# One matmul of 512 columns in place of two of 256 in four of seven Strassen steps: a decoder layer on Trainium2

## The chip, the cores and the metric

The kernel runs on one core of one Trainium2 chip. Its time is the device time of one execution in microseconds (us). Before the change three runs gave 1889.41, 1891.42 and 1900.57 us; the median is 1891.42 us. All data is float32, and the matmuls take their operands as `fp32r`, a form of float32 that TensorE reads directly. Every large product is made of three passes: each operand is split into a high part (rounded to `fp32r`) and a low part (what is left), and the product is high times high, plus high times low, plus low times high.

## The reference

One decoder layer over 512 tokens of width 2048: multi-head latent attention, a LayerNorm over the residual sum, then a dense MLP and another LayerNorm.

```python
h = layer_norm(ALPHA * h + mla_mixer(h, ...), ln_g[0, 0], ln_b[0, 0])
h = layer_norm(ALPHA * h + square(relu(h @ w1)) @ w2, ln_g[0, 1], ln_b[0, 1])
# h: 512 x 2048, w1: 2048 x 8192 (the up product), w2: 8192 x 2048 (the down product)
```

The change lies in the product of `h` with `w1`, called the up product here.

## The kernel before

The program runs in stages: the attention and its projections, the first LayerNorm (together the first third of the time), then the up product from about 592 us to 1237 us, then the down product and the second LayerNorm. There is no scheduler: the order of the work on each engine is the order in which the code writes it, and the engines meet through semaphores. TensorE (PE), VectorE (DVE) and ScalarE (ACT) each work through their own list and stop at the first wait that isn't met.

**The up product.** The 8192 columns of `w1` are taken in 32 pairs of 256 columns, that is two blocks of 128. The first two pairs are plain products. The other 30 (`UP_PAIRS - PLAIN`) use the Strassen-Winograd scheme: seven block products, steps 0 to 6, where a plain 2 x 2 block product needs eight. In one step a left operand (a block of `h`, or a sum of blocks, 1024 deep and 256 tokens wide, in SBUF as a high part `up_hi` and a low part `up_lo`) meets a weight block of 1024 x 128 (high part in `w_hi`, low part in `w_lo`, four slots each). The 1024 deep sum is eight chunks of 128 (`HK`), with three matmuls of 256 columns to a chunk (`product`, lines 1580, 1584 and 1585), so a step is 24 matmuls. The weights are the stationary operand, the tokens the moving one. The results of steps 0, 2, 4 and 6 add up in the one PSUM bank `i % 2`, step 1 goes to bank 2, steps 3 and 5 to bank 3.

**Around it, once per pair.**
- SyncE loads the four weight blocks b11, b12, b21, b22 (`up_loads`). DVE makes four sums of them (`up_t1` to `up_t4`, lines 1201 to 1219).
- ACT rounds each step's weights to `w_hi` (`up_weights`, line 701), and DVE subtracts to get `w_lo` (`up_rest`, line 1184). PE starts a step when its `w_lo` is there.
- ACT copies three partial results from PSUM into `kept` (`keep_product`, line 724): bank `i % 2` after step 0 and after step 2, and bank 3 after step 3. PE waits for them before step 2, step 4 and step 5, since those steps write over what is copied.
- DVE adds the final sums into `hidden` (`c_block`, line 1227, three times). The fourth block, c21, is what stands in bank `i % 2` after step 6: ACT applies the Relu as it reads it (`c21`, line 729).
- ACT applies Relu to the other three blocks (line 734, 768 columns) and squares all four (line 740, 1024 columns). DVE then makes the four sums and differences that the down product needs (`hidden_sums`, lines 1232 to 1237). ACT rounds seven blocks to `h_hi` (`hidden_hi`, line 747, 1792 columns) and stores it, DVE makes `h_lo` (`hidden_lo`, line 1244), and ACT issues its store. This work on pair i - 1 is done while PE is in pair i.

The functions that the change touches follow; `(i, n)` is the pair and the number of the part.

Of the kernel before, what the change touches and what calls it, by code (L numbers as in the profile page):

```python
# [4 lines left out]
P = 128  # L5
# [44 lines left out]
STEPS = 7  # L50
# [52 lines left out]
def mla_mlp_program(nc, xT, x, w, w_up, w_down, const, gain, ln, out):  # L103
# [3 lines left out]
    with ExitStack() as ctx:  # L107
# [69 lines left out]
        up_act = [None] * STEPS  # L177
        for step, left in enumerate(STEP_OF):
            up_act[left] = tuple(sb(f"up_{part}{left}", [P, HK, HT], f32r, at=base + (UP_ACT_AT[step] + 8 * i) * KB)
                                 for i, part in enumerate(("hi", "lo")))  # L180
# [11 lines left out]
        kept = sb("kept", [P, 3, HT], at=base + 144 * KB)  # L192
# [63 lines left out]
        p_kept, c21_made, c_made = sem("p_kept"), sem("c21_made"), sem("c_made")  # L256
        h_relu, h_made, h_sums = sem("h_relu"), sem("h_made"), sem("h_sums")
# [243 lines left out]
        def _(act):  # L501
# [219 lines left out]
            def keep_product(i, n, of, after):  # L721

                act.wait_ge(up_unit, up_steps(i, after - 1))
                act.activation(kept[:, n, :], of[:, 0:HT], ACT.Copy).then_inc(p_kept, 1)

            def c21(i):

                act.wait_ge(up_unit, up_steps(i, STEPS - 1))
                act.activation(hidden[:, 0, :], bank[:, i % 2, 0:HT], ACT.Relu).then_inc(c21_made, 1)

            def relu_hidden(i):

                act.wait_ge(c_made, 3 * (i - PLAIN) + 3)
                act.activation(hidden[:, 1:4, :], hidden[:, 1:4, :], ACT.Relu).then_inc(h_relu, 1)

            def square_hidden(i):

                act.wait_ge(h_relu, i - PLAIN + 1)
                act.wait_ge(c21_made, i - PLAIN + 1)
# [24 lines left out]
            def up_pair(i):  # L764

                relu_hidden(i - 1)
                c21(i - 1)
                square_hidden(i - 1)
                act.wait_ge(up_t_made, 4 * (i - PLAIN) + 3)
                up_weights(i, 2, b11[i % 2])  # L770
                act.wait_ge(up_t_made, 4 * (i - PLAIN) + 2)
                up_weights(i, 3, b12)
                keep_product(i, 0, bank[:, i % 2, :], 1)
# [7 lines left out]
                keep_product(i, 1, bank[:, i % 2, :], 3)  # L781
                act.wait_ge(up_t_made, 4 * (i - PLAIN) + 4)
                up_weights(i, 6, b21[i % 2])
                keep_product(i, 2, bank[:, 3, :], 4)
# [10 lines left out]
            def plain_pairs():  # L795
# [27 lines left out]
                keep_product(PLAIN, 0, bank[:, 0, :], 1)  # L823
# [6 lines left out]
                keep_product(PLAIN, 1, bank[:, 0, :], 3)  # L830
# [5 lines left out]
                keep_product(PLAIN, 2, bank[:, 3, :], 4)  # L836
# [73 lines left out]
            for n in range(4):  # L910
                down_weights(0, n)
            relu_hidden(last)
            c21(last)
# [306 lines left out]

# [863 lines left out]
```

## Time and profile before

| | before |
|---|---|
| median of three runs | 1891.42 us |
| profiled execution, its own time | 1892.82 us |
| span of the profile | 1890.7 us |
| PE busy | 1837.9 us (97%), 11120 matmuls |
| DVE busy | 1366.3 us (72%) |
| ACT busy | 889.1 us (47%) |
| mean granted TensorE clock | 0.991 |

The span goes from the first to the last instruction of the profiled execution. PE is busy when any matmul is between its start and its modelled end; matmuls are pipelined, so neighbours overlap, and what a matmul takes of PE's time is the distance from its start to the next one's start, not its duration. The same holds for DVE and ACT to a lesser degree: the next instruction starts a little before the last one's recorded end. The clock column PEclk gives the granted clock as a share of 2.4 GHz.

### The profile page before, as it was taken

What the parts mean: (1) busy time and instruction counts of PE and PEld (TensorE: products, weight loads), DVE (VectorE), ACT (ScalarE), POOL (GpSimd) and SP (SyncE); (2) the same over time, 40 slices, a digit from 0 to 9 for tenths busy, and PEclk for the clock granted to TensorE, in tenths of its full rate; (3) what the DMA queues carried; (4) which work ended last, traced back from release to release, by engine and by line L of the source; (5) the groups of instructions that cost most, each with busy time, mean ns of one, the idle gap of its engine ahead of it and who ended that gap; (6) DMA issues with size and microseconds to landing.
All of it is one profiled execution on the core that took longest, in us unless ns stands there. A gap on an engine that the chain in (4) does not pass through costs nothing.

```text
span 1890.7 us, 28438 instructions
## 1 busy us (share of the span) xinstructions
PE 1837.9 (97%) x11120; PEld 1647.0 (87%) x11120; DVE 1366.3 (72%) x1680; ACT 889.1 (47%) x1136; POOL 282.9 (15%) x118
## 2 busy tenths in 40 slices
PE   8999999999999999999999999989999999999994
PEld 6889898988888999999999999977887888788883
DVE  3054545521128888888888888878999999999997
ACT  5255655532217656656656556533433334333434
POOL 5342232324431000000000000000111122100003
PEclk9999999999999999999999999999999999999998
DMA  6222111133234564564564554686465564654812
GB/s 225 79 80 77 56 67 55 67 138 107 100 139 147 172 223 172 195 221 167 200 216 167 206 210 167 221 317 265 174 236 202 196 254 179 234 221 170 319 67 89
DMA packets 112719, 321.30 MB, mean 170 GB/s; under 512 B 7184, under 2 KB 64656, under 8 KB 95760
## 3 DMA queue, kind: packets, MB, share of 16 engines
q1 hardware_dynamic: 53280, 256.92, 36.2%
q10 hardware_dynamic: 59376, 63.59, 10.1%
q8 instruction: 32, 0.52, 0.1%
q14 instruction: 31, 0.25, 0.0%
HBM read 253.38 MB, written 67.11 MB: 170 GB/s over the span
## 4 chain that ended last, share of the span: by engine, by line
PE 86%; DVE 7%; issue 3%; DMA 1%; ACT 1%; POOL 1%; SPq 0%; POOLq 0%; ACTq 0%; DVEq 0%
PE bank L1580 28%; PE bank L1584 28%; PE bank L1585 28%; DVE w_lo L1312 2%; DMA d_b<-down_weights 1%; DVE acc L1372 1%; PE bank L1726 1%; DVE d_b L1347 1%; POOL w_lo L453 0%; DVE acc L1382 0%; PE bank L1612 0%; POOL acc L497 0%; ACT acc L935 0%; PE bank L1821 0%; PE bank L1718 0%
## 5 line engine op out<-in xcount | busy, mean ns | idle before, releaser
L1580 PE MATMUL bank<-up_hi,w_hi 128*128 128x256 f32 x1808 | 512.6, 284 | 3.2 <-DVE w_lo L1190 2.8
L1584 PE MATMUL bank<-up_lo,w_hi 128*128 128x256 f32 x1808 | 512.3, 283 | 0.0
L1585 PE MATMUL bank<-up_hi,w_lo 128*128 128x256 f32 x1808 | 512.3, 283 | 0.0
L1580 PE MATMUL bank<-w_hi,down_act 128*128 128x512 f32 x896 | 352.0, 393 | 13.6 <-DVE w_lo L1312 5.9
L904 ACT ACTIVATE w_hi<-d_b 128x1024 fp32r<-128x1024 f32 x192 | 201.5, 1060 | 321.8 <-PE bank L1585 251.9
L1580 PEld LDWEIGHTS bank<-up_hi,w_hi 128*128 128x128 f32 x1808 | 347.6, 192 | 3.9 <-DVE w_lo L1190 3.3
L1584 PE MATMUL bank<-w_lo,down_act 128*128 128x512 f32 x896 | 350.0, 391 | 0.0
L1585 PE MATMUL bank<-w_hi,down_act 128*128 128x512 f32 x896 | 349.9, 390 | 0.0
L1585 PEld LDWEIGHTS bank<-up_hi,w_lo 128*128 128x128 f32 x1808 | 347.8, 192 | 0.0
L1584 PEld LDWEIGHTS bank<-up_lo,w_hi 128*128 128x128 f32 x1808 | 347.8, 192 | 0.0
L1312 DVE TENSOR_TENSOR w_lo<-d_b,w_hi 128x1024 fp32r<-128x1024 f32 x190 | 251.7, 1359 | 24.1 <-ACT w_hi L904 24.1
L701 ACT ACTIVATE w_hi<-up_b 128x1024 fp32r<-128x1024 f32 x180 | 187.0, 1054 | 159.4 <-PE bank L1585 131.7
L453 POOL TENSOR_TENSOR w_lo<-raw,w_hi 128x1024 fp32r<-128x1024 f32 x82 | 198.0, 2417 | 355.5 <-ACT w_hi L510 355.3
L1580 PEld LDWEIGHTS bank<-w_hi,down_act 128*128 128x128 f32 x896 | 169.0, 189 | 56.8 <-issue 14.5
L1184 DVE TENSOR_TENSOR w_lo<-up_b,w_hi 128x1024 fp32r<-128x1024 f32 x180 | 216.9, 1218 | 1.4 <-ACT w_hi L701 1.4
L1585 PEld LDWEIGHTS bank<-w_hi,down_act 128*128 128x128 f32 x896 | 168.9, 189 | 35.4
L1584 PEld LDWEIGHTS bank<-w_lo,down_act 128*128 128x128 f32 x896 | 168.9, 189 | 34.2
L478 POOL TENSOR_TENSOR residual<-residual,ln_rows 128x1024 f32<-128x1024 f32 x8 | 36.2, 4525 | 1002.4 <-DMA residual<-rows_kept 1002.4
L510 ACT ACTIVATE w_hi<-raw 128x1024 fp32r<-128x1024 f32 x82 | 86.7, 1058 | 148.2 <-PE bank L1580 115.6
L1372 DVE TENSOR_TENSOR acc<-acc,bank 128x512 f32<-128x512 f32 x202 | 130.0, 679 | 12.4 <-PE bank L1585 12.1
L1138 DVE SCALAR_TENSOR_TENSOR rows<-rows,bank 128x512 f32<-128x512 f32 x16 | 11.0, 686 | 136.5 <-PE bank L1585 136.5
L1580 PE MATMUL bank<-w_hi,act_hi 128*128 128x512 f32 x256 | 99.9, 390 | 0.0
(168 smaller groups left out, 2782.0 us busy)
## 6 DMA issues: line engine op xcount, KB each, us to landing
up_b<-up_weights SPq DMA_DIRECT2D x128, 512.0 KB, 4.8
d_b<-down_weights SPq DMA_DIRECT2D x64, 1024.0 KB, 5.3
down_act<-acts_kept SPq DMA_DIRECT2D x56, 1024.0 KB, 5.0
raw<-weights SPq DMA_DIRECT2D x82, 512.0 KB, 3.2
acts_kept<-h_hi ACTq DMA_DIRECT2D x32, 896.0 KB, 5.8
acts_kept<-h_lo ACTq DMA_DIRECT2D x32, 896.0 KB, 6.6
x_raw<-x_t SPq DMA_DIRECT2D x8, 512.0 KB, 7.7
rows<-x_rows ACTq DMA_DIRECT2D x4, 1024.0 KB, 7.9
```

Of the source, the lines that this page charges most:

```text
L453: pool.tensor_tensor(w_lo[:, s, :], raw[:, s % RAWS, :], w_hi[:, s, :].bitcast(f32), ALU.subtract)\
L478: pool.tensor_tensor(part, part, ln_rows[:, 0, cols], ALU.mult).then_inc(residual_gained, 1)
L510: act.activation(w_hi[:, s, :], raw[:, s % RAWS, :], ACT.Copy).then_inc(w_hi_made, 1)
L701: act.activation(w_hi[:, UP_SLOT[u], :], source[:, :], ACT.Copy).then_inc(up_hi, 1)
L904: act.activation(w_hi[:, DOWN_SLOT[n], :], source[:, ab, :], ACT.Copy).then_inc(down_hi, 1)
L1184: dve.tensor_tensor(w_lo[:, s, :], source[:, :], w_hi[:, s, :].bitcast(f32), ALU.subtract).then_inc(up_lo, 1)
L1312: dve.tensor_tensor(w_lo[:, DOWN_SLOT[n], :], source[:, ab, :], w_hi[:, DOWN_SLOT[n], :].bitcast(f32), ALU.subtract).then_inc(made, 1)
L1347: dve.tensor_tensor(d_b11[:, ab, :], d_t3[:, ab, :], d_b11[:, ab, :], ALU.add).then_inc(down_t_made, 1)
L1372: dve.tensor_tensor(part, part, of, ALU.add).then_inc(evicted, 1)
L1580: first_pass = pe.matmul(out_, a_hi, b_hi, start=start, stop=False, skip_group_check=more)
L1584: pe.matmul(out_, a_hi, b_lo, start=False, stop=False, skip_group_check=more)
L1585: return pe.matmul(out_, a_lo, b_hi, start=False, stop=stop, skip_group_check=more)
```

## The change

In steps 0, 2, 4 and 6 the high weights now pass once over both parts of the left operand. The two parts already lie one after the other in SBUF, so a tensor `up_both` names them as one, and a single matmul of 512 columns writes high times high into the lower half of the PSUM bank and high times low into the upper half. The low weights then pass over the high part alone, into the lower half, as before. A chunk of such a step is so two matmuls (512 and 256 columns) instead of three of 256. Steps 1, 3 and 5 stay as they were.

The two halves of bank `i % 2` have to be added. ACT now copies the upper half to `kept` after steps 0, 2 and 6 (`keep_half`, in place of the two copies of the whole result and of the Relu of c21), and DVE adds the lower half to it: `keep_halves(i, 0)` after step 0, `keep_halves(i, 1)` after step 2, `c21` after step 6. In `c_block(i, 1)` after step 4 DVE first adds the upper half to the kept product of step 3 and then the lower half. PE waits for `keep_halves` where it waited for the copy. The Relu on ACT takes all four blocks.

```diff
-            def keep_product(i, n, of, after):
-                act.wait_ge(up_unit, up_steps(i, after - 1))
-                act.activation(kept[:, n, :], of[:, 0:HT], ACT.Copy).then_inc(p_kept, 1)
-
-            def c21(i):
-                act.wait_ge(up_unit, up_steps(i, STEPS - 1))
-                act.activation(hidden[:, 0, :], bank[:, i % 2, 0:HT], ACT.Relu).then_inc(c21_made, 1)
+            def keep_p5(i):
+                act.wait_ge(up_unit, up_steps(i, 3))
+                act.activation(kept[:, 2, :], bank[:, 3, 0:HT], ACT.Copy).then_inc(p_kept, 1)
+
+            def keep_half(i, n):
+                act.wait_ge(up_unit, up_steps(i, (0, 2, 6)[n]))
+                act.activation(kept[:, (0, 1, 3)[n], :], bank[:, i % 2, HT:2 * HT], ACT.Copy).then_inc(half_kept, 1)
             def relu_hidden(i):
                 act.wait_ge(c_made, 3 * (i - PLAIN) + 3)
-                act.activation(hidden[:, 1:4, :], hidden[:, 1:4, :], ACT.Relu).then_inc(h_relu, 1)
+                act.wait_ge(c21_made, i - PLAIN + 1)
+                act.activation(hidden[:, 0:4, :], hidden[:, 0:4, :], ACT.Relu).then_inc(h_relu, 1)
...
             def up_pair(i):
-                relu_hidden(i - 1)
-                c21(i - 1)
-                square_hidden(i - 1)
+                keep_half(i - 1, 2)
                 act.wait_ge(up_t_made, 4 * (i - PLAIN) + 3)
                 up_weights(i, 2, b11[i % 2])
+                relu_hidden(i - 1)
+                square_hidden(i - 1)
+                keep_half(i, 0)
                 act.wait_ge(up_t_made, 4 * (i - PLAIN) + 2)
                 up_weights(i, 3, b12)
-                keep_product(i, 0, bank[:, i % 2, :], 1)
                 hidden_hi(i - 1)
...
+            keep_half(last, 2)
             relu_hidden(last)
-            c21(last)
             square_hidden(last)
...
+            def keep_halves(i, n):
+                dve.wait_ge(half_kept, 3 * (i - PLAIN) + n + 1)
+                dve.tensor_tensor(kept[:, n, :], kept[:, n, :], bank[:, i % 2, 0:HT], ALU.add).then_inc(halves_kept, 1)
             def c_block(i, n):
                 dve.wait_ge(up_unit, up_steps(i, after - 1))
-                dve.wait_ge(p_kept, 3 * (i - PLAIN) + keeps)
+                if n == 1:
+                    dve.wait_ge(p_kept, i - PLAIN + 1)
+                    dve.tensor_tensor(kept[:, 2, :], bank[:, of, HT:2 * HT], kept[:, 2, :], ALU.add).then_inc(c22_half, 1)
+                    dve.wait_ge(c22_half, i - PLAIN + 1)
+                else:
+                    dve.wait_ge(halves_kept, 2 * (i - PLAIN) + keeps)
                 dve.tensor_tensor(hidden[:, at, :], bank[:, of, 0:HT], kept[:, keep, :], ALU.add).then_inc(c_made, 1)
+            def c21(i):
+                dve.wait_ge(half_kept, 3 * (i - PLAIN) + 3)
+                dve.tensor_tensor(hidden[:, 0, :], kept[:, 3, :], bank[:, i % 2, 0:HT], ALU.add).then_inc(c21_made, 1)
...
             for i in range(PLAIN, UP_PAIRS):
                 ahead = i < UP_PAIRS - 1
                 if i > PLAIN:
+                    up_rest(i, 2)
+                    keep_halves(i, 0)
                     hidden_sums(i - 1)
-                    up_rest(i, 2)
                     up_rest(i, 3)
                     hidden_lo(i - 1)
                     up_rest(i, 4)
...
                 c_block(i, 0)
                 if i > PLAIN:
                     up_t4(i)
+                    keep_halves(i, 1)
                     up_rest(i, 5)
...
                     c_block(i, 2)
                     up_t2(i + 1)
+                    c21(i)
                     up_rest(i + 1, 1)
                 else:
                     c_block(i, 2)
+                    c21(i)
                     down_rest(0, 0)
                     down_t3(0)
...
             def up_products(u, parity, ready=None):
+                    if u in (1, 3, 5):
+                        last = product(bank[:, b, 0:HT], w_hi[:, s, cols], w_lo[:, s, cols], a_hi[:, k, :], a_lo[:, k, :],
+                                       u in (1, 3) and k == 0, k == HK - 1, more)
+                    else:
+                        pe.matmul(bank[:, b, :], w_hi[:, s, cols], up_both[STEP_OF[u]][:, :, k, :],
+                                  start=u == 0 and k == 0, stop=k == HK - 1, skip_group_check=True)
+                        last = pe.matmul(bank[:, b, 0:HT], w_lo[:, s, cols], a_hi[:, k, :], start=False, stop=k == HK - 1,
+                                         skip_group_check=True)
                 last.then_inc(up_unit, 1)
...
-                pe.wait_ge(p_kept, 3 * (i - PLAIN) + 1)
+                pe.wait_ge(halves_kept, 2 * (i - PLAIN) + 1)
                 up_products(2, parity, (up_act_lo, 6) if first else None)
...
-                pe.wait_ge(p_kept, 3 * (i - PLAIN) + 2)
+                pe.wait_ge(halves_kept, 2 * (i - PLAIN) + 2)
                 up_products(4, parity, (up_act_lo, 12) if first else None)
```

The order on ACT from the end of one pair into the next. Before, the Relu and the Square of the finished pair come first, and the first copy to `kept` stands after both weights:

```order
L734 ACTIVATE hidden<-hidden 128x768
L729 ACTIVATE hidden<-bank 128x256
L740 ACTIVATE hidden<-hidden 128x1024
L701 ACTIVATE w_hi<-up_b_0_101 128x1024
L701 ACTIVATE w_hi<-up_b_98 128x1024
L724 ACTIVATE kept<-bank 128x256
L747 ACTIVATE h_hi<-hidden 128x1792
```

And in the change:

```order
L731 ACTIVATE kept<-bank 128x256
L702 ACTIVATE w_hi<-up_b_0_94 128x1024
L737 ACTIVATE hidden<-hidden 128x1024
L742 ACTIVATE hidden<-hidden 128x1024
L731 ACTIVATE kept<-bank 128x256
L702 ACTIVATE w_hi<-up_b_91 128x1024
L749 ACTIVATE h_hi<-hidden 128x1792
```

The rounding of step 2's weights moved ahead of the Relu and the Square, and the copy after step 0 ahead of step 3's weights.

The order on DVE over the same place, up to the sum `up_t4` (line 1219) and what follows it. Before:

```order
L1232 TENSOR_TENSOR hidden<-hidden 128x256
L1233 TENSOR_TENSOR hidden<-hidden 128x256
L1235 TENSOR_TENSOR hidden<-hidden 128x256
L1237 TENSOR_TENSOR hidden<-hidden 128x256
L1184 TENSOR_TENSOR w_lo<-up_b_1_104,w_hi 128x1024
L1184 TENSOR_TENSOR w_lo<-up_b_98,w_hi 128x1024
L1244 TENSOR_TENSOR h_lo<-hidden,h_hi 128x1792
L1184 TENSOR_TENSOR w_lo<-up_t_99,w_hi 128x1024
L1227 TENSOR_TENSOR hidden<-bank,kept 128x256
L1219 TENSOR_TENSOR up_b_1_105<-up_b_1_105,up_b_1_104 128x1024
L1184 TENSOR_TENSOR w_lo<-up_b_1_103,w_hi 128x1024
```

In the change line 1227 is `keep_halves`, lines 1236 and 1240 are `c_block`, and line 1221 is `up_t4`; step 2's `w_lo` stands just ahead of the first row:

```order
L1227 TENSOR_TENSOR kept<-kept,bank 128x256
L1250 TENSOR_TENSOR hidden<-hidden 128x256
L1251 TENSOR_TENSOR hidden<-hidden 128x256
L1253 TENSOR_TENSOR hidden<-hidden 128x256
L1255 TENSOR_TENSOR hidden<-hidden 128x256
L1186 TENSOR_TENSOR w_lo<-up_b_91,w_hi 128x1024
L1262 TENSOR_TENSOR h_lo<-hidden,h_hi 128x1792
L1186 TENSOR_TENSOR w_lo<-up_t_92,w_hi 128x1024
L1240 TENSOR_TENSOR hidden<-bank,kept 128x256
L1221 TENSOR_TENSOR up_b_0_95<-up_b_0_95,up_b_0_94 128x1024
L1227 TENSOR_TENSOR kept<-kept,bank 128x256
L1186 TENSOR_TENSOR w_lo<-up_b_1_96,w_hi 128x1024
```

The two `keep_halves` are new. The second one, for which PE waits before step 4, stands behind the whole row of work on the pair before, behind step 4's `w_lo` and behind `up_t4`.

The order on DVE where the up product ends, in the change (line 1330 is the down product's `down_rest`, line 1343 its `down_t3`):

```order
L1236 TENSOR_TENSOR kept<-bank,kept 128x256
L1240 TENSOR_TENSOR hidden<-bank,kept 128x256 x2
L1245 TENSOR_TENSOR hidden<-kept,bank 128x256
L1330 TENSOR_TENSOR w_lo<-d_b_114,w_hi 128x1024 x2
L1343 TENSOR_TENSOR d_t_117<-d_b_0_115,d_b_113 128x1024 x2
```

The new c21 (line 1245) stands ahead of the down product's first low weights; before, these followed the last `c_block` directly.

## Rows read from the trace of the kernel before

**Rows 1.** The page's first part: busy us, share of the span and instructions.

```profile
PE 1837.9 (97%) x11120; PEld 1647.0 (87%) x11120; DVE 1366.3 (72%) x1680; ACT 889.1 (47%) x1136; POOL 282.9 (15%) x118
```

**Rows 2.** Windows, up product: us; busy PE, PEld, DVE, ACT, POOL; clock; DMA share; GB/s.

```profile
700.00:1200.00 500.00, 500.00 (x4169) 500.00 (x4168) 424.45 (x473) 294.06 (x348) 0.00 (x0) 1.00 0.56 196
```

**Rows 3.** Timeline of PE: 256 columns 24 matmuls apart; 512 columns 9 apart.

```profile
start us, us, engine line op out<-in xcount [idle before <-releaser]
1014.92 0.28 PE L1580 MATMUL bank<-up_hi,w_hi 128*128 128x256 f32 x1
...
1017.80 0.28 PE L1580 MATMUL bank<-up_hi,w_hi 128*128 128x256 f32 x1
...
449.87 0.39 PE L1585 MATMUL bank<-w_hi,act_lo 128*128 128x512 f32 x1
...
451.91 0.39 PE L1585 MATMUL bank<-w_hi,act_lo 128*128 128x512 f32 x1
```

**Rows 4.** Timeline of ACT from the end of one pair into the next.

```profile
1015.12 0.38 ACT L729 ACTIVATE hidden<-bank 128x256 f32<-128x256 f32 x1 [1.03 <-PE bank L1585]
1015.60 1.06 ACT L740 ACTIVATE hidden<-hidden 128x1024 f32<-128x1024 f32 x1
1016.57 1.99 ACT L701 ACTIVATE w_hi<-up_b 128x1024 fp32r<-128x1024 f32 x2
1018.46 0.36 ACT L724 ACTIVATE kept<-bank 128x256 f32<-128x256 f32 x1
1018.72 1.69 ACT L747 ACTIVATE h_hi<-hidden 128x1792 fp32r<-128x1792 f32 x1
```

**Rows 5.** Timeline of DVE over the same stretch.

```profile
1016.69 0.43 DVE L1232 TENSOR_TENSOR hidden<-hidden 128x256 f32<-128x256 f32 x1 [1.75 <-ACT hidden L740]
...
1017.82 0.42 DVE L1237 TENSOR_TENSOR hidden<-hidden 128x256 f32<-128x256 f32 x1
1018.16 2.35 DVE L1184 TENSOR_TENSOR w_lo<-up_b,w_hi 128x1024 fp32r<-128x1024 f32 x2
1020.44 2.02 DVE L1244 TENSOR_TENSOR h_lo<-hidden,h_hi 128x1792 fp32r<-128x1792 f32 x1
1022.39 1.22 DVE L1184 TENSOR_TENSOR w_lo<-up_t,w_hi 128x1024 fp32r<-128x1024 f32 x1
1023.52 0.41 DVE L1227 TENSOR_TENSOR hidden<-bank,kept 128x256 f32<-128x256 f32 x1
1023.86 1.21 DVE L1219 TENSOR_TENSOR up_b<-up_b,up_b 128x1024 f32<-128x1024 f32 x1
```

**Rows 6.** Timeline where PE waits for a `w_lo` and starts again.

```profile
586.30 2.36 DVE L1190 TENSOR_TENSOR w_lo<-up_b,w_hi 128x1024 fp32r<-128x1024 f32 x2 [3.94 <-ACT w_hi L693]
...
587.58 0.19 PEld L1580 LDWEIGHTS bank<-up_hi,w_hi 128*128 128x128 f32 x1 [2.89 <-DVE w_lo L1190]
587.59 0.39 PE L1580 MATMUL bank<-up_hi,w_hi 128*128 128x256 f32 x1 [2.65 <-DVE w_lo L1190]
...
587.81 0.28 PE L1584 MATMUL bank<-up_lo,w_hi 128*128 128x256 f32 x1
```

**Rows 7.** The page's DMA issues: count, KB each, us to landing.

```profile
up_b<-up_weights SPq DMA_DIRECT2D x128, 512.0 KB, 4.8
```

**Rows 8.** Timeline of ACT and DVE where the down product begins.

```profile
1236.94 2.01 ACT L904 ACTIVATE w_hi<-d_b 128x1024 fp32r<-128x1024 f32 x2 [1.81 <-PE bank L1585]
...
1234.35 2.35 DVE L1312 TENSOR_TENSOR w_lo<-d_b,w_hi 128x1024 fp32r<-128x1024 f32 x2
1239.64 1.23 DVE L1325 TENSOR_TENSOR d_t<-d_b,d_b 128x1024 f32<-128x1024 f32 x1 [2.95 <-DMA d_b<-down_weights]
```

**Rows 9.** Windows behind the wait of Rows 6, and around one of 1.63 us.

```profile
588.00:592.00 4.00, 4.00 (x24) 4.00 (x24) 3.65 (x7) 3.04 (x5) 0.00 (x0) 0.60 0.91 290
...
1283.00:1287.00 4.00, 2.37 (x11) 1.72 (x10) 4.00 (x6) 2.00 (x2) 0.00 (x0) 1.00 0.57 240
```

**Rows 10.** Timeline of PE: that wait of 1.63 us.

```profile
1284.94 0.50 PE L1580 MATMUL bank<-w_hi,down_act 128*128 128x512 f32 x1 [1.63 <-DVE w_lo L1312]
```

More of the change, by code:

```diff
@@ L174, in mla_mlp_program @@
         rows = sb("rows", [P, TT, D], at=base + 80 * KB)
-        up_act = [None] * STEPS
+        up_act, up_both = [None] * STEPS, [None] * STEPS
         for step, left in enumerate(STEP_OF):
-            up_act[left] = tuple(sb(f"up_{part}{left}", [P, HK, HT], f32r, at=base + (UP_ACT_AT[step] + 8 * i) * KB)
-                                 for i, part in enumerate(("hi", "lo")))
+            up_both[left] = sb(f"up_act{left}", [P, 2, HK, HT], f32r, at=base + UP_ACT_AT[step] * KB)
+            up_act[left] = up_both[left][:, 0], up_both[left][:, 1]
         a21 = up_act[S3]
@@ L780, in up_pair @@
                 store_hidden(i - 1, 1)
-                keep_product(i, 1, bank[:, i % 2, :], 3)
+                keep_half(i, 1)
                 act.wait_ge(up_t_made, 4 * (i - PLAIN) + 4)
                 up_weights(i, 6, b21[i % 2])
-                keep_product(i, 2, bank[:, 3, :], 4)
+                keep_p5(i)
                 if i < UP_PAIRS - 1:
@@ L822, in plain_pairs @@
                 up_weights(PLAIN, 3, b12)
[L823 removed]
+                keep_half(PLAIN, 0)
                 hidden_hi(0)
@@ L829, in plain_pairs @@
                 store_hidden(0, 1)
-                keep_product(PLAIN, 1, bank[:, 0, :], 3)
+                keep_half(PLAIN, 1)
                 plain_square(1)
@@ L1504, in _ @@
             up_rest(PLAIN, 3)
+            keep_halves(PLAIN, 0)
             hidden_lo(0)
@@ L1508, in _ @@
             up_rest(PLAIN, 5)
+            keep_halves(PLAIN, 1)
             hidden_sums(1)
@@ L1846, in up_products @@
                 a_hi, a_lo = up_act[STEP_OF[u]]
-                dst = bank[:, (parity, 2, parity, 3, parity, 3, parity)[u], 0:HT]
+                b = (parity, 2, parity, 3, parity, 3, parity)[u]
+                more = u in (2, 4, 5, 6)
                 for k in range(HK):
@@ L1851, in up_products @@
                     cols = slice(P * k, P * k + P)
-                    last = product(dst, w_hi[:, s, cols], w_lo[:, s, cols], a_hi[:, k, :], a_lo[:, k, :],
-                                   u in (0, 1, 3) and k == 0, k == HK - 1, u in (2, 4, 5, 6))
+                    if u in (1, 3, 5):
[6 more added lines that the diff above has]
+                                         skip_group_check=True)
                 last.then_inc(up_unit, 1)
```

10 lines of the change are left out of this document (5 added, 5 removed).

## The prediction, made before the changed kernel was run

> **What bounds the kernel now.** I read the page's busy shares first: PE is busy for 97% of the span, DVE for 72%, ACT for 47% [rows 1]. An average over stages decides nothing, so the windows of the up product came next. In the 500 us from 700 to 1200 PE has no gap at all, at full clock, while DVE works 85% of the time and ACT 59% [rows 2]. There only the distance between two matmuls counts, and the timeline of PE gives it. Matmuls of 256 columns: 24 of them start in 2.88 us, 0.120 us each, and that is one step. Matmuls of 512 columns: 9 in 2.04 us, 0.227 us each [rows 3]. One pair is seven steps, 7 x 2.88 = 20.16 us. Last I laid the timelines of ACT and DVE beside it, since the change puts DVE between PE and PE [rows 4, 5]. DVE is idle for 1.75 us before `hidden_sums`, as it waits for the Square; then it has unbroken work up to `up_t4`. The slack there is large: step 4's `w_lo` is done at 1022.39 + 1.22 = 1023.61, and step 4 begins on PE at 1014.92 + 4 x 2.88 = 1026.44. PE waits for nobody because each thing it needs comes more than a microsecond early. So the question is whether this stays true.
>
> **PE's own work.** A merged pair of matmuls costs 0.227 in place of 0.240 us. The price is from contiguous moving operands; in the change the 512 columns are two runs of 256. That form is not in the trace. Its lower bound is 0.227 us; the upper bound is that nothing is gained, 0.240 us. I take 0.227, since it is the row of the same column count. A changed step has eight chunks of 0.227 + 0.120 us: 2.77 us, 0.11 us less than 2.88. Four such steps make 0.44 us a pair, 13.2 us in 30 pairs. That is all the change can give: 0.7% of the time.
>
> The Trainium skill ("TensorE: Matmul & The Clock Gate", Back-to-back issue gap) gives a warm matmul N / 2.4 ns plus a fixed 2.5 ns, so a merge would save only 2.5 ns: 30 x 32 x 2.5 ns = 2.4 us in all, an estimate from that page. The trace does not agree, as 256 columns take 120 ns where the rule gives 109; by the rule the changed step would be 2.86 us and my sum below 1929 us.
>
> **DVE's and ACT's work.** DVE gets four more additions of 256 columns in a pair: two `keep_halves`, a second one in `c_block(i, 1)`, and c21, which was ACT's. Each holds DVE for 0.34 us (1023.52 to 1023.86, [rows 5]), 1.4 us together with 0.1 us for the addition that waits for the one ahead. DVE's busy 0.85 x 20.16 = 17.1 us becomes 18.6, and PE's pair would be 19.72. So DVE is not full. ACT trades a Relu and three copies for four copies and gets a wider Relu: nearly nothing, hidden by its 40% of idle time. By busy time alone the change would win.
>
> **The new chain.** PE may start step 4 only when `keep_halves(i, 1)` is done, and that stands on DVE behind everything that belongs to the pair before, as the order of DVE in the change shows. I walk it with starts from [rows 4, 5]. Time 0 is 1015.12, when a pair's step 6 has released ACT; PE's next pair starts at -0.20 (1014.92).
> - ACT: copy of the half at 0.00. The next instruction follows a copy after 0.26 (1018.46 to 1018.72): step 2's `w_hi` at 0.26. Two `w_hi` are 0.945 apart: Relu at 1.21. It is now 1024 columns wide, which I price as the Square, 1.06 us: end 2.27. The Square waits for it, 0.10 after its end (1015.50 to 1015.60): 2.37. What follows the Square comes 0.97 later: the copy after step 0 at 3.34, end 3.72. Step 0 ended at 2.77, so PE isn't what it waits for.
> - DVE: meanwhile c21 at 0.41, step 1's `w_lo` at 0.75 (done 1.97, wanted at 2.57), step 2's `w_lo` at 1.88. Then it waits for that copy: `keep_halves(i, 0)` at 3.75, and `hidden_sums` at 4.09. Before, they began at 1.57: 2.5 us later, of which 1.1 is a `w_lo` that moved ahead. The four take 1.55 to the end of the last (1016.69 to 1018.24): 5.64.
> - ACT: `h_hi` at 5.67, 1.69 long, end 7.36. Before, it began at 3.60. DVE did two `w_lo` while it ran; now one is left to do (5.56 to 6.69), and DVE stands still until 7.39.
> - DVE: `h_lo` at 7.39; 1.95 later (1020.44 to 1022.39) step 4's `w_lo` at 9.34; 1.13 later `c_block(i, 0)` at 10.47; 0.34 later `up_t4` at 10.81; 1.13 later `keep_halves(i, 1)` at 11.94. With the 0.42 us of such an addition it ends at 12.36.
> - PE: the only start after a wait in this stage shows the weight load 0.06 after the `w_lo` (first of two, 586.30 + 1.22 = 587.52, to 587.58), the matmul 0.01 later, and the second matmul 0.22 behind it in place of 0.12 [rows 6]. Step 4 starts at 12.43 and loses 0.10.
>
> Without the wait it would start at -0.20 + 2.77 + 2.88 + 2.77 + 2.88 = 11.10. **PE stands 12.43 + 0.10 - 11.10 = 1.43 us in each pair**, 0.44 is saved, and the net is +0.99 us. It does not work itself off: every link from 0.00 on hangs on the end of step 6, so the next pair starts the same walk. Steps 4 to 6 take 8.42 us and DVE catches up: after `keep_halves` come three long instructions, step 6's `w_lo` being done at 15.76, wanted at 18.2.
>
> Other waits stay hidden. Step 2 wants `keep_halves(i, 0)` at 5.45, it ends at 4.17. Step 4's own `w_lo` ends at 10.56. Step 3's `w_lo` ends at 6.78, and SyncE loads the next b12 behind it; with the usual 4.8 us [rows 7] it is there at 11.6, and `up_t3` uses it at 13.41. If that cover were gone, DVE would be later by the same amount.
>
> Pair 2 is without the work on a Strassen pair before and with slack, so I give it 0.1 us of gain. The other 29 pairs cost 29 x 0.99 = 28.7 us.
>
> **The end of the up product.** ACT has two roundings for the down product ahead of the last half copy [rows 8]: copy at 1.90, end 2.28; c21 on DVE at 2.31; only then the down product's first `w_lo`, at 2.65, done at 3.87. It was at 1234.35, ahead of the step's end. So PE stands about 4 us, but much of it comes out of the waits that follow. What carries on is DVE: `down_t3` began at 1239.64, 2.70 after the release at 1236.94, as its transfer landed. Now two `w_lo` stand ahead, and it begins at 2.65 + 2.27 = 4.92. I charge the difference, 2.2 us; the bounds are 0 (waits for later transfers take it up) and 4.
>
> **Sum.** The profiled execution took 1892.82 us with a span of 1890.7; 1892.8 + 28.7 + 2.2 - 0.1 = 1923.6. It stood 1.4 us above the median, 1891.42, which is noise here. **Forecast: 1924 us**, 1.7% slower.
>
> **Rivals.**
> - *The chain is the bound as walked* (0.72): 1924. Some twelve links with an error of a few hundredths each, all in a line, and 29 pairs: 0.3 us a pair either way, 1914 to 1934.
> - *The wait does not arise and PE stays the bound* (0.09), the other side: DVE reaches `keep_halves(i, 1)` in time. This needs 1.43 us less between step 6 and that addition; the sign turns already where 0.99 us is missing. The place is the stretch from the Square to `h_lo`, where ACT and DVE wait for each other twice (3.75 and 7.39) and where my starts are worked out, not seen. For it: DVE has 6% of idle time left. Against it: of the links, all but the Relu's width stand in the trace with the same operands. Time: 1892.8 - 13.2 + 2.2 = 1882.
> - *The chain is about 1 us shorter* (0.06): saving and wait cancel, 1895.
> - *The merged matmul gains nothing* (0.08), because its operand lies in two runs: steps 4 and 6 are 0.11 longer each while the chain stays, +1.21 us a pair: 1930.
> - *The clock falls in the waits* (0.05). After the wait of 2.65 us [rows 6] the granted clock over the next 4 us was 0.60 [rows 9], which costs 1.6 us. After one of 1.63 us [rows 10] it stayed at 1.00 [rows 9]. Mine are about 1.2 us of real gap, so likely not. If each did, 29 x 1.6 = 46 us more: 1970.
>
> The Trainium skill (same page, A second HAM failure mode: psum-queue depth-cycling) describes a kernel whose short stops between groups of matmuls let the clock swing again and again. Single stops of this length in this trace don't show it; no run so far has them in series.
>
> **Range and chances.** The first case holds 1914 to 1934, the fourth lies in it, and reaching toward the third and the second until 2 in 10 are left out gives 1908 to 1938. About 1% is what a measurement of this kernel can tell from no change, so the borders are 1872 and 1910. The gain is capped at 0.7%: faster 0.02. Same: the second and third cases and the low tail of the first, 0.17. Slower 0.81.
>
> **What would show it.** Per pair one gap on PE before step 4, released by the `keep_halves` line on DVE; a distance of 21.15 us between pairs where 20.16 stood; the 512 column matmul 0.227 us ahead of the next; DVE idle twice in a pair, for ACT's copy and for `h_hi`; full clock in the windows. I am wrong if PE is still unbroken from 700 to 1200, if its gap stands before another step, or if the clock is below 1.00 there.

## The result, and the profile after

The changed kernel took 1927.17 us (median of 4 runs, 1924.56 to 1930.70), the kernel before 1892.39 us beside it (4 runs): 1.0177 times as long, 95% interval 1.0154 to 1.0199. Forecast were 1924 us. The profiled execution took 1928.11 us with a span of 1925.9, 35.2 us more than the span before. Ratios here and below are of fast runs alone, which leaves out one slow execution of 4699.45 us, of the kernel without the additions of halves.

The page's busy shares come first, as in [rows 1]:

```profile
PE 1839.7 (96%) x10160; PEld 1598.3 (83%) x10160; DVE 1409.8 (73%) x1800; ACT 896.1 (47%) x1136; POOL 276.9 (14%) x118
```

PE has 960 matmuls less (30 pairs x 32) and DVE 120 additions more (30 x 4), as the diff says. PE's share hardly fell, and nothing here points to a loss of 35 us. The window that answers to [rows 2] does (busy us of PE, PEld, DVE, ACT, POOL; granted clock; DMA share; GB/s):

```profile
700.00:1200.00 500.00, 476.12 (x3216) 436.65 (x3216) 439.12 (x545) 285.10 (x329) 0.00 (x0) 1.00 0.54 189
```

Before, PE was busy for all of these 500 us; now it stands still for 23.9 of them. The clock stayed at 1.00. The table of waits names the cause (engine, line, releaser: us in all, times, longest us):

```profile
PE bank L1883 <- DVE kept L1227: 29.3, 29, 1.4
DVE h_lo L1262 <- ACT h_hi L749: 19.6, 30, 1.2
DVE kept L1227 <- ACT kept L731: 17.4, 30, 0.8
```

L1227 is the addition in `keep_halves`, L1883 the merged matmul. There is one gap in each of 29 pairs, always before step 4: 1.44 us in the first and 0.98 to 1.00 in the rest. The page's chain of waits shows the same turn, by engine (before, PE had 86% of it, DVE 7%):

```profile
PE 68%; DVE 15%; ACT 8%; issue 6%; DMA 2%; POOL 1%; POOLq 0%; SPq 0%; ACTq 0%; DVEq 0%
```

Now the walk of one pair, the timelines of ACT and DVE that answer to [rows 4, 5]. ACT:

```profile
1033.71 0.38 ACT L731 ACTIVATE kept<-bank 128x256 f32<-128x256 f32 x1 [1.71 <-PE bank L1885]
1033.99 1.05 ACT L702 ACTIVATE w_hi<-up_b 128x1024 fp32r<-128x1024 f32 x1
1034.94 1.05 ACT L737 ACTIVATE hidden<-hidden 128x1024 f32<-128x1024 f32 x1
1036.02 1.06 ACT L742 ACTIVATE hidden<-hidden 128x1024 f32<-128x1024 f32 x1
1036.99 0.36 ACT L731 ACTIVATE kept<-bank 128x256 f32<-128x256 f32 x1
...
1039.31 1.71 ACT L749 ACTIVATE h_hi<-hidden 128x1792 fp32r<-128x1792 f32 x1 [1.01 <-DVE hidden L1255]
```

DVE:

```profile
1037.38 0.42 DVE L1227 TENSOR_TENSOR kept<-kept,bank 128x256 f32<-128x256 f32 x1 [0.57 <-ACT kept L731]
1037.72 0.42 DVE L1250 TENSOR_TENSOR hidden<-hidden 128x256 f32<-128x256 f32 x1
...
1041.05 2.03 DVE L1262 TENSOR_TENSOR h_lo<-hidden,h_hi 128x1792 fp32r<-128x1792 f32 x1 [0.64 <-ACT h_hi L749]
1042.99 1.22 DVE L1186 TENSOR_TENSOR w_lo<-up_t,w_hi 128x1024 fp32r<-128x1024 f32 x1
1044.12 0.42 DVE L1240 TENSOR_TENSOR hidden<-bank,kept 128x256 f32<-128x256 f32 x1
1044.46 1.22 DVE L1221 TENSOR_TENSOR up_b<-up_b,up_b 128x1024 f32<-128x1024 f32 x1
1045.59 0.42 DVE L1227 TENSOR_TENSOR kept<-kept,bank 128x256 f32<-128x256 f32 x1
```

And PE on both sides of the gap:

```profile
1044.78 0.28 PE L1609 MATMUL bank<-up_act,w_lo 128*128 128x256 f32 x1
1046.06 0.50 PE L1883 MATMUL bank<-up_act,w_hi 128*128 128x512 f32 x1 [1.00 <-DVE kept L1227]
```

Starts in us after step 6's release (1033.71 here), against the walk in the prediction:

| | Relu | Square | copy | `keep_halves` 0 | first sum | `h_hi` | `h_lo` | step 4's `w_lo` | c(i,0) | `up_t4` | `keep_halves` 1 | PE |
|---|---|---|---|---|---|---|---|---|---|---|---|---|
| forecast | 1.21 | 2.37 | 3.34 | 3.75 | 4.09 | 5.67 | 7.39 | 9.34 | 10.47 | 10.81 | 11.94 | 12.43 |
| measured | 1.23 | 2.31 | 3.28 | 3.67 | 4.01 | 5.60 | 7.34 | 9.28 | 10.41 | 10.75 | 11.88 | 12.35 |

Each link is within 0.08 us. The idle 0.57 us on DVE before `keep_halves` 0 and the 0.64 us before `h_lo` are the two places where ACT and DVE wait for each other in turn. Between the first and the last of these gaps the pairs stand (1257.79 - 665.40) / 28 = 21.16 us apart; 21.15 were forecast.

To place the rest, I split each profiled execution in three by PE's own rows: the lead to the end of the wait near 588 us, the up product from there to the start of its last matmul, and what follows the end of that matmul. The up product takes 678.2 us (before 649.0, +29.2), what follows takes 659.4 us (before 653.8, +5.6), and the lead makes the last 0.4. Forecast were +28.6 and +2.2. These are single profiles: three kernels here with the same up product have 678.2, 679.9 and 679.7 us, and the granted clock between 588 and 600 us differs among them.

The 5.6 us behind the up product can be split once more. PE stands 5.1 us right behind the up product, where it had no gap before, and its waits from there to the end of the down product add up to 17.7 us (before 13.6, +4.1). The rest of that stretch is 1.9 us longer, as matmuls start further apart, and what comes behind it is 0.4 us shorter. When PE starts again, the granted clock is near the lower of its two levels (1.2 GHz), and it was 1.00 at that place before:

```profile
1272.00:1276.00 4.00, 4.00 (x11) 3.09 (x11) 4.00 (x5) 0.62 (x1) 0.00 (x0) 0.54 1.03 422
```

In the down product the clock falls so after three waits (5.12, 1.99 and the second of two of 2.80 us), before after two (3.70 and 2.80 us).

### The profile page after: what moved, and what is told of

The parts are those of the page before. It is cut to its first block, busy times and chain, and to the rows that moved or that the text cites. A ratio compares the mean times of both kernels' runs of the same rounds, so it can differ in the third digit from the quotient of the medians.

```text
span 1925.9 us, 26638 instructions
## 1 busy us (share of the span) xinstructions
PE 1839.7 (96%) x10160; PEld 1598.3 (83%) x10160; DVE 1409.8 (73%) x1800; ACT 896.1 (47%) x1136; POOL 276.9 (14%) x118
## 4 chain that ended last, share of the span: by engine, by line
PE 68%; DVE 15%; ACT 8%; issue 6%; DMA 2%; POOL 1%; POOLq 0%; SPq 0%; ACTq 0%; DVEq 0%
PE bank L1604 19%; PE bank L1608 19%; PE bank L1609 19%; PE bank L1883 6%; PE bank L1885 3%; ACT h_hi L749 3%; DVE h_lo L1262 3%; DVE w_lo L1330 2%; DVE up_b L1221 2%; ACT hidden L737 2%; DVE kept L1227 1%; DMA d_b<-down_weights 1%; ACT w_hi L702 1%; DVE acc L1390 1%; PE bank L1750 1%
## 5 line engine op out<-in xcount | busy, mean ns | idle before, releaser
L1883 PE MATMUL bank<-up_act,w_hi 128*128 128x512 f32 x960 | 345.2, 401 | 29.3 <-DVE kept L1227 29.3
L1885 PE MATMUL bank<-up_act,w_lo 128*128 128x256 f32 x960 | 269.2, 280 | 0.0
L1604 PE MATMUL bank<-up_act,w_hi 128*128 128x256 f32 x848 | 240.6, 284 | 3.4 <-DVE w_lo L1192 2.8
L1883 PEld LDWEIGHTS bank<-up_act,w_hi 128*128 128x128 f32 x960 | 180.4, 188 | 75.1 <-DVE kept L1227 33.5
L1608 PE MATMUL bank<-up_act,w_hi 128*128 128x256 f32 x848 | 240.4, 284 | 0.0
L1609 PE MATMUL bank<-up_act,w_lo 128*128 128x256 f32 x848 | 240.3, 283 | 0.0
L1885 PEld LDWEIGHTS bank<-up_act,w_lo 128*128 128x128 f32 x960 | 181.4, 189 | 0.0
L479 POOL TENSOR_TENSOR residual<-residual,ln_rows 128x1024 f32<-128x1024 f32 x8 | 30.1, 3768 | 1043.5 <-DMA residual<-rows_kept 1043.5
L1604 PEld LDWEIGHTS bank<-up_act,w_hi 128*128 128x128 f32 x848 | 161.9, 191 | 8.3 <-DVE w_lo L1192 3.3
L1609 PEld LDWEIGHTS bank<-up_act,w_lo 128*128 128x128 f32 x848 | 162.3, 191 | 0.0
L1608 PEld LDWEIGHTS bank<-up_act,w_hi 128*128 128x128 f32 x848 | 162.1, 191 | 0.0
```

The source lines that it names most:

```text
L1604: first_pass = pe.matmul(out_, a_hi, b_hi, start=start, stop=False, skip_group_check=more)
L1608: pe.matmul(out_, a_hi, b_lo, start=False, stop=False, skip_group_check=more)
L1609: return pe.matmul(out_, a_lo, b_hi, start=False, stop=stop, skip_group_check=more)
L1883: pe.matmul(bank[:, b, :], w_hi[:, s, cols], up_both[STEP_OF[u]][:, :, k, :], start=u == 0 and k == 0, stop=k == HK - 1, skip_group_check= ...
L1885: last = pe.matmul(bank[:, b, 0:HT], w_lo[:, s, cols], a_hi[:, k, :], start=False, stop=k == HK - 1, skip_group_check=True)
```

## Experiments

Ratios are against the kernel before, in runs of the same chip. The rival that remained after the profile was throughput: DVE, ACT and PE are all so busy in a pair that any order would leave a gap. The chain theory says that one late addition costs all of it.

**The addition ahead of `up_t4`.** `keep_halves(i, 1)` needs nothing of `up_t4`; it only stands behind it. The change with two lines swapped:

```diff
-                    up_t4(i)
                     keep_halves(i, 1)
+                    up_t4(i)
```

> The change with one swap on VectorE: the addition of the halves of step 2 stands ahead of up_t4 instead of behind it. Chain theory (step 4 waits for that addition, and for nothing else): the addition starts one 1024 column instruction, 1.13 us, earlier in each pair; the wait on PE shrinks from 1.00 us of gap to about nothing or a few tenths, the distance between pairs goes from 21.16 to about 20.0 us, and with 29 pairs the time falls by some 33 us to 1894 (1889 to 1899). Rival, VectorE simply has too much work (the order does not matter, since the same instructions run): no change, 1927.

Measured: 1899.92 us against 1894.52, 1.0025 (1.0004 to 1.0046), just above the range of the expectation. The window from 700 to 1200:

```profile
700.00:1200.00 500.00, 500.00 (x3394) 461.44 (x3393) 462.24 (x575) 301.72 (x350) 0.00 (x0) 1.00 0.56 197
```

PE is unbroken, while DVE works 92% of the time, more than in the change. So the engines are not full and the rival falls: 1.13 us less in the line of DVE takes away the whole gap. The up product takes 644.5 us, 4.5 less than before. What keeps the whole slower lies behind it: 667.9 us in this profile, before 653.8. There PE waits 6.1 us at the end of the up product, and three times 2.8 us in the down product; both are taken up below.

**The same addition ahead of `c_block(i, 0)` too.**

```diff
+                if i > PLAIN:
+                    keep_halves(i, 1)
                 dve.wait_ge(h_lo_made, i)
                 c_block(i, 0)
                 if i > PLAIN:
                     up_t4(i)
-                    keep_halves(i, 1)
```

> The same addition one place further ahead, before c_block(i, 0) too, 1.47 us earlier than in the change. Chain theory: no gap on PE before step 4 is left, PE is the bound again with its merged steps, pairs 19.8 us apart, 29 x 1.36 = 39 us less than the change, 1888 (1884 to 1893); what is left above 1882 is the end of the up product, untouched here. Rival, too much work on VectorE: 1927, or at best a pair as long as its 18.6 us of work plus its waits for ScalarE, with gaps on PE in other places.

Measured: 1898.33 us, 1.0020 (1.0002 to 1.0038). PE is unbroken again. The distance of two pairs is that of these rows on DVE, 19.99 us:

```profile
1003.01 0.41 DVE L1227 TENSOR_TENSOR kept<-kept,bank 128x256 f32<-128x256 f32 x1
...
1023.00 0.41 DVE L1227 TENSOR_TENSOR kept<-kept,bank 128x256 f32<-128x256 f32 x1
```

Forecast were 19.72 in the prediction for a pair without a gap, and 1888 (1884 to 1893) for this run: a miss. The chain is gone, and yet a pair gains 0.17 us on the 20.16 before and not 0.44. Most of the miss is the size of the merge's gain, which the experiments below measure. A small part is a next wait. Before step 5 PE needs ACT's copy of bank 3, and that now ends at 1006.25, 0.06 us before step 5's weight load:

```profile
1005.88 0.37 ACT L725 ACTIVATE kept<-bank 128x256 f32<-128x256 f32 x1
...
1006.31 0.19 PEld L1605 LDWEIGHTS bank<-up_act,w_hi 128*128 128x128 f32 x1
```

The first two matmuls of step 5 then stand 0.17 us apart in place of 0.12; the table of busy times calls PE unbroken all the same. The up product takes 644.1 us, 4.8 less than before, but the whole is no faster than before; what follows it is 4.5 us longer (658.3).

**The merge undone, the rest of the change kept.** Two matmuls of 256 columns in place of the merged one; the first high product of step 0's first chunk is left out.

```diff
-                        pe.matmul(bank[:, b, :], w_hi[:, s, cols], up_both[STEP_OF[u]][:, :, k, :],
+                        pe.matmul(bank[:, b, 0:HT], w_hi[:, s, cols], a_hi[:, k, :],
+                                  start=u == 0 and k == 0, stop=k == HK - 1, skip_group_check=True)
+                        pe.matmul(bank[:, b, HT:2 * HT], w_hi[:, s, cols], a_lo[:, k, :],
                                   start=u == 0 and k == 0, stop=k == HK - 1, skip_group_check=True)
```

> The change with its merged matmul undone alone: high times high and high times low are again two matmuls of 256 columns, into the two halves of the bank; all copies, additions and waits of the change stay. Chain theory: steps 0 and 2 run beside the chain, so their length is hidden; only steps 4 and 6 lie on the path, 0.07 to 0.11 us longer each, 29 x 0.18 = 5 us: 1932. Rival, the merged matmul with its operand in two runs gains nothing: 1927. If all four steps were on the path: 29 x 0.36 = 10 us, 1937.

Measured: 1930.41 us, 1.0189 (1.0158 to 1.0220). PE's waits:

```profile
PE bank L1883 <- DVE kept L1227: 25.4, 29, 1.2
```

The gap shrank from 1.00 to 0.86 us and the pair grew from 21.16 to 21.28. PE's step 4 is set by the chain, so what the merge saves in steps 0 and 2 is only waited for; what it saves in steps 4 and 6 counts. In 29 pairs that is 3.5 us; the single profile has an up product longer by 2.0 us, and I had expected 5. Inside the change the merge is worth about 0.12 us a pair. The medians (1.0189 with 1.0158 to 1.0220, the change 1.0177) can't tell this from nothing; the distance of the pairs can.

**The additions of halves left out.** `keep_halves` gives up its two sums, so the halves are not joined there; PE and `c_block` wait for ACT's copies instead.

```diff
-                dve.wait_ge(half_kept, 3 * (i - PLAIN) + n + 1)
-                dve.tensor_tensor(kept[:, n, :], kept[:, n, :], bank[:, i % 2, 0:HT], ALU.add).then_inc(halves_kept, 1)
+                pass
...
-                pe.wait_ge(halves_kept, 2 * (i - PLAIN) + 2)
+                pe.wait_ge(half_kept, 3 * (i - PLAIN) + 2)
```

> The change without the two additions keep_halves (those parts of the sum are left out of the output); PE waits for ScalarE's copy of the half instead. Chain theory: ScalarE's copy after step 2 is done about 1 us before step 4 can start, so the gap goes: 1886 (1882 to 1892). Rival A, step 4's low weights are late too, the addition being only the last of two: a smaller gap stays, 1895 or more. Rival B, the merged matmul costs PE more than two single ones: well above 1892 with PE unbroken.

Measured: 1893.35 us, 0.9996 (0.9981 to 1.0011):

```profile
700.00:1200.00 500.00, 500.00 (x3413) 462.66 (x3412) 448.72 (x527) 304.17 (x352) 0.00 (x0) 1.00 0.56 198
```

Without the wait PE is unbroken and the pair is 19.93 us. The gap needs this addition. What is then left of the change as a gain is 0.23 us a pair, half of the forecast 0.44, and the median is just above the range of the expectation.

**The end of the up product reordered.** On ACT the last half copy goes ahead of the down product's third and fourth rounding, on DVE `c21` behind its first `w_lo`; the change is otherwise as it was.

```diff
-            for n in range(4):
+            for n in range(2):
                 down_weights(0, n)
             keep_half(last, 2)
+            for n in range(2, 4):
+                down_weights(0, n)
...
-                    c21(i)
                     down_rest(0, 0)
+                    c21(i)
```

> The change with only the end of the up product reordered: ScalarE copies the last half ahead of the third and fourth rounding for the down product, and VectorE makes the down product's first low weights ahead of c21. Theory (this order costs the down product its start): PE's gap of 5.1 us right behind the up product becomes shorter, and down_t3 begins when its transfer lands, some 4.4 us after the last step instead of 6.1; the span behind the up product's last matmul, 659.4 us in the change and 653.8 before, falls by about 2 us. Median 1925 (1922 to 1928). Rival (the transfers of the down product's weights are what is late): no change, 1927. The gaps of 1.00 us in the pairs stay in either case.

Measured: 1921.18 us against 1891.98, 1.0150 (1.0128 to 1.0171). The gaps in the pairs stay. In the change the end looks as follows, ACT, then DVE, then PE:

```profile
1267.64 2.00 ACT L906 ACTIVATE w_hi<-d_b 128x1024 fp32r<-128x1024 f32 x2 [2.78 <-DMA d_b<-down_weights]
1269.56 0.36 ACT L731 ACTIVATE kept<-bank 128x256 f32<-128x256 f32 x1
```

```profile
1269.95 0.42 DVE L1245 TENSOR_TENSOR hidden<-kept,bank 128x256 f32<-128x256 f32 x1 [5.78 <-ACT kept L731]
1270.29 2.35 DVE L1330 TENSOR_TENSOR w_lo<-d_b,w_hi 128x1024 fp32r<-128x1024 f32 x2
1272.56 2.35 DVE L1343 TENSOR_TENSOR d_t<-d_b,d_b 128x1024 f32<-128x1024 f32 x2
```

```profile
1266.25 0.28 PE L1885 MATMUL bank<-up_act,w_lo 128*128 128x256 f32 x1
1271.65 0.76 PE L1604 MATMUL bank<-w_hi,down_act 128*128 128x512 f32 x1 [5.12 <-DVE w_lo L1330]
```

ACT's roundings themselves waited for a transfer until 1267.64, so the copy behind them came about 1.0 us later than I had walked it. `down_t3` (L1343) starts 6.0 us after the last up step ended (1266.53); before it was 2.8 (1236.84 to 1239.64), so it is 3.2 us later, not 2.2. In the reordered kernel, on DVE:

```profile
1269.92 1.22 DVE L1332 TENSOR_TENSOR w_lo<-d_b,w_hi 128x1024 fp32r<-128x1024 f32 x1
1271.70 0.42 DVE L1247 TENSOR_TENSOR hidden<-kept,bank 128x256 f32<-128x256 f32 x1 [0.56 <-ACT kept L731]
1275.17 2.36 DVE L1345 TENSOR_TENSOR d_t<-d_b,d_b 128x1024 f32<-128x1024 f32 x2 [3.04 <-DMA d_b<-down_weights]
```

PE goes into the down product without a gap, and `down_t3` starts 3.9 us after the last step, when its transfer has landed. What follows the up product takes 650.3 us, 9.1 less than in the change. Here 2.1 us of `down_t3`'s delay come back, and two waits of 2.8 us in the down product, of which the experiments on GpSimd below tell, do not occur in it. That the median lies just below the expected 1922 to 1928 fits this, but one profile doesn't show it for all four runs.

**Both edits together.** The edits are those of the second and the fifth experiment:

```diff
+                if i > PLAIN:
+                    keep_halves(i, 1)
...
+            for n in range(2):
...
+                    c21(i)
```

> Both edits together: the addition of the halves of step 2 ahead of c_block(i, 0), as in the run with it alone, and the reordered end. Theory: 4.9 us gained in the up product against the kernel before, as there, and about 3 us lost behind it instead of 4.6: a ratio to the kernel before of 0.999 (0.996 to 1.001), which can't be told from no change. Rival (the end doesn't matter): 1.002 as with the first edit alone.

Measured: 1890.91 us against 1891.98, 0.9998 (0.9985 to 1.0010). The up product takes 642.4 us, the rest 651.8. Both losses of the change are gone; the gain that is left can't be told from none by this measurement.

**The 512 columns as one run.** In that kernel the high and low parts of a left operand are laid side by side for each chunk, so that the merged matmul reads 512 columns in one piece:

```diff
-            up_both[left] = sb(f"up_act{left}", [P, 2, HK, HT], f32r, at=base + UP_ACT_AT[step] * KB)
...
+                whole = sb(f"up_act{left}", [P, HK, 2, HT], f32r, at=base + UP_ACT_AT[step] * KB)
+                up_act[left] = whole[:, :, 0, :], whole[:, :, 1, :]
```

> The kernel with both edits, and the high and low parts of the left operands of steps 0, 2, 4 and 6 laid out chunk by chunk, so that the 512 columns of a merged matmul lie in one run instead of two. In the change a merged matmul held PE for 0.236 us, where contiguous ones of 512 columns took 0.227. Theory A, the two runs cost the 9 ns: 0.227 here, a step of 2.77 us instead of 2.82; since the addition of the halves is then again a little late, the pair shortens by 0.1 us only, 3 us in all. Theory B, the 9 ns belong to the alternation of 512 and 256 columns or to the up product's place in memory: 0.236 as before, no change of the time.

Measured: 1891.09 us, 0.9994 (0.9978 to 1.0009). First PE in the change, in two runs, then here in one:

```profile
1040.25 0.40 PE L1883 MATMUL bank<-up_act,w_hi 128*128 128x512 f32 x1
1040.49 0.28 PE L1885 MATMUL bank<-up_act,w_lo 128*128 128x256 f32 x1
1040.61 0.40 PE L1883 MATMUL bank<-up_act,w_hi 128*128 128x512 f32 x1
```

```profile
1020.33 0.40 PE L1891 MATMUL bank<-up_act,w_hi 128*128 128x512 f32 x1
1020.57 0.28 PE L1893 MATMUL bank<-up_act,w_lo 128*128 128x256 f32 x1
1020.69 0.40 PE L1891 MATMUL bank<-up_act,w_hi 128*128 128x512 f32 x1
```

The merged matmul holds PE for 0.236 us (median of 960, in both layouts) and not for 0.227; the one behind it for 0.117. Chunks stand 0.353 us apart in both layouts, where three of 256 columns take 0.360. The two runs are not the cause.

**The merge undone where nothing waits.** The kernel with both edits, with two matmuls in place of the merged one again:

```diff
-                        pe.matmul(bank[:, b, :], w_hi[:, s, cols], up_both[STEP_OF[u]][:, :, k, :],
+                        pe.matmul(bank[:, b, 0:HT], w_hi[:, s, cols], a_hi[:, k, :],
                                   start=u == 0 and k == 0, stop=k == HK - 1, skip_group_check=True)
+                        pe.matmul(bank[:, b, HT:2 * HT], w_hi[:, s, cols], a_lo[:, k, :],
+                                  start=False, stop=k == HK - 1, skip_group_check=True)
```

> The kernel with both edits, its merged matmul taken apart again into two of 256 columns (same copies, additions and waits). This measures the merge alone where PE is the bound. By the matmul distances of the traces (0.236 against 0.240) the merge is worth 32 x 6.5 ns a pair: steps of 2.88 us, pairs of 20.16 instead of 19.99, 29 x 0.17 = 5 us slower than with the merge. By the estimate of the prediction it would be 13 us. Rival (an additional cost of the new additions on PE, as PSUM is read while it is written): pairs longer than 20.16.

Measured: 1895.45 us, 1.0017 (1.0002 to 1.0033), with steps of 2.88 us throughout. Its up product is 649.0 us, that of the two kernels with the merge 642.4: the merge is worth 6.6 us there, and 4.4 us in the medians (1895.45 against 1891.09 beside it). By the chunks, 30 pairs x 32 chunks x 0.007 us (0.360 - 0.353) is 6.7; 13.2 were forecast. The pairs stand 20.16 us apart, against 19.99 with the merge and its small wait before step 5, and no longer, so the new additions cost PE nothing of their own.

**GpSimd's work in the down product cut down, in the change and in the kernel before.** Three more places of 2.8 us wanted explaining: PE waits so twice in the change's down product and once before. In the change, GpSimd, DVE and PE at one of them:

```profile
1552.55 2.40 POOL L479 TENSOR_TENSOR residual<-residual,ln_rows 128x1024 f32<-128x1024 f32 x1 [27.27 <-DMA residual<-rows_kept]
1555.03 3.26 POOL L485 TENSOR_TENSOR residual<-residual,ln_rows 128x1024 f32<-128x1024 f32 x1
```

```profile
1549.18 2.36 DVE L1330 TENSOR_TENSOR w_lo<-d_b,w_hi 128x1024 fp32r<-128x1024 f32 x2
...
1552.65 6.72 DVE L1330 TENSOR_TENSOR w_lo<-d_b,w_hi 128x1024 fp32r<-128x1024 f32 x2
```

```profile
1565.24 0.49 PE L1604 MATMUL bank<-w_hi,down_act 128*128 128x512 f32 x1 [2.80 <-DVE w_lo L1330]
```

The pair of `w_lo` that began 0.10 us after GpSimd took 6.72 us in place of 2.36. The test leaves the residual's rows unscaled and without bias, save for 8 columns, in both kernels:

```diff
-                pool.tensor_tensor(part, part, ln_rows[:, 0, cols], ALU.mult).then_inc(residual_gained, 1)
+                pool.tensor_tensor(part[:, 0:8], part[:, 0:8], ln_rows[:, 0, 0:8], ALU.mult).then_inc(residual_gained, 1)
...
```

> The change with GpSimd's two operations on the residual rows in the down product cut from 1024 columns to 8 (the rest of these rows is left unscaled and without its bias). Theory (the part of the loss behind the up product that the order of its end doesn't explain comes from GpSimd: when its two operations fall on VectorE's two low weights, these take 6.7 us instead of 2.4 and PE waits 2.8 us, twice in the change and once before): no w_lo group above 2.4 us and no wait of 2.8 us in the down product, and the span behind the up product's last matmul falls from 659.4 us by at least 5.6. Rival (the waits come from the transfers of the weights): they stay.

> The kernel before with the same cut in GpSimd's operations. Theory: its one wait of 2.8 us goes too, and the span behind the up product's last matmul is then shorter than in the change with this cut by the 3.4 us by which down_t3 begins later there, no longer by 5.6; the medians of the two differ by 29.2 + 3.4 = 32.6 us (30 to 35). Rival (the change loses more in the down product for another reason): the difference behind the up product stays at 5.6 us or more.

Measured, against 1895.10 us for the whole kernel before: the change so cut 1917.98 us, 1.0116 (1.0097 to 1.0135); the kernel before so cut 1885.92 us, 0.9948 (0.9933 to 0.9964). In the first, DVE where GpSimd starts beside it:

```profile
1476.61 2.36 DVE L1330 TENSOR_TENSOR w_lo<-d_b,w_hi 128x1024 fp32r<-128x1024 f32 x2
```

No `w_lo` is slowed and no wait of 2.8 us is left. What follows the up product takes 647.6 and 645.3 us: of the 5.6 us between the two kernels 2.3 remain, where I had expected 3.4. So some 3 us of the change's loss go with a second such collision, that is, with where the shifted work happened to meet GpSimd; this rests on one profile of each kernel. Both kernels got shorter by more than their waits of 2.8 us (11.8 and 8.5 us), which I have not taken apart. The difference of the medians is 32.1 us.

## Why the prediction was right, and where not

- **What bounds it, and the new chain: right.** PE was unbroken before, the wait arises where forecast, and it does not work itself off: every walk begins with the release by step 6. The first two experiments and the one without the sums show that this one wait is the cause. The up product lost 29.2 us; 28.6 were forecast.
- **The gain of the merge: half as large.** The term of 0.227 us was mis-sized: 0.236 beside a matmul of 256 columns that takes 0.117, so 0.007 us a chunk and not 0.013. I had taken the row of 512 columns among others of 512 [rows 3], a neighbourhood that the change doesn't have. The Trainium skill ("TensorE: Matmul & The Clock Gate", Back-to-back issue gap) would give 2.5 ns for each matmul saved, an estimate from its formula for a single warm matmul; measured were 7, so the rule was too low here and my row too high.
- **Why the sum held all the same: in part luck.** In pair time the miss is 0.44 - 0.23 = 0.21 us, some 6 us in 29 pairs. Half of it lies in steps 0 and 2, ahead of the wait, and comes off the wait: from the start that it would have had without one (1044.78 + 0.12 = 1044.90) step 4 comes 1.16 us late, where 1.33 were forecast. That half would have come off in any case, by the mechanism. The other half was met by the chain, 0.08 us shorter than walked, mostly because the Square followed the Relu's end after 0.03 us and not 0.10: two errors that cancel. The net was forecast as 0.99 us and is 1.00.
- **The end of the up product: right in place, its 2.2 us met by luck.** `down_t3` came 3.2 us later in place of 2.2. The step that failed is the copy at 1.90: I had let ACT's two roundings start at the release, and they waited about 1.0 us for a transfer of their own. With GpSimd's work cut down only 2.3 us reach the end of the program, within the bounds of 0 and 4, so the charge of 2.2 is right in its sum and not in its parts. The prediction also had no price for the clock here, which stood at 0.54 from 1272 to 1276, behind the wait of 5.1 us. Added to it comes the second collision of GpSimd and DVE, which the prediction did not have. Together 5.6 us in place of 2.2: most of the 3 us by which the median stands above 1924.
- **The rivals.** No wait (1882) and cancelling (1895): refuted, with 29 gaps. Merge worth nothing (1930): it is worth half, and undoing it inside the change gave 1930.41. The clock: 1.00 in the window, with 29 stops of 1.0 us; where it did fall is behind longer waits outside the pairs. The Trainium skill (same page, A second HAM failure mode: psum-queue depth-cycling) describes swings of the clock from short stops in series; stops of 1.0 us, 21.16 us apart, do not show them here.
- **Open:** why a matmul of 512 columns takes 0.236 us between those of 256: the layout is excluded, nothing else was tried. Nor is it known why the transfer for ACT's roundings at the end of the up product came late. That other waits of the down product fall differently in the reordered kernels (650.3 us against 647.6 to 659.4) was seen, not taken apart.

## What to carry to other kernels

Before work is moved from the bounding engine to another, write down the order on the receiving engine and walk from the last release to the new wait: a 0.4 us addition cost 1 us in each pair with DVE only 88% busy, because of what stood ahead of it. An addition that releases the bounding engine goes ahead of everything that only fills buffers; here moving one line gave back about 29 of the 35 us. It did not make the change a gain: the best of its kernels, with both edits, measured 0.9998 and 0.9994 of the kernel before, which can't be told from no change. And price a merged instruction among the neighbours that it will have, since the issue time of a kind is not the same in every mixture.

## What was not expected of the hardware

- Matmuls in alternation: 512 columns 0.236 us and 256 columns 0.117, against 0.227 and 0.120 in rows of their own kind. Why is open.
- VectorE and GpSimd slow each other, and a difference of 0.1 us in their starts decides who pays. GpSimd 0.10 us ahead, in the kernel before: two `w_lo` take 6.72 us in place of 2.36, GpSimd's multiplication 2.40.

```profile
1439.50 2.40 POOL L478 TENSOR_TENSOR residual<-residual,ln_rows 128x1024 f32<-128x1024 f32 x1 [27.25 <-DMA residual<-rows_kept]
...
1439.60 6.72 DVE L1312 TENSOR_TENSOR w_lo<-d_b,w_hi 128x1024 fp32r<-128x1024 f32 x2
```

  When both start at the same moment, DVE's row is unchanged and GpSimd's takes over 8 us, while DVE runs five instructions of 1024 columns without a break:

```profile
1521.46 8.04 POOL L478 TENSOR_TENSOR residual<-residual,ln_rows 128x1024 f32<-128x1024 f32 x1 [27.37 <-DMA residual<-rows_kept]
...
1521.46 2.35 DVE L1312 TENSOR_TENSOR w_lo<-d_b,w_hi 128x1024 fp32r<-128x1024 f32 x2
```
